# Two transformer blocks in one kernel: the residual stream of the second expert pass, the output projection and the FFN accumulated with tokens instead of features on the partitions

## The reference, cut to what matters

```python
# first block, end: PEER experts, then the final norm of the block
act = gelu(einsum("td,thkd->thk", xb, expert_down[idx]))
x = x + einsum("thk,thkd->td", gate * act, expert_up[idx])
x = rmsnorm(x, norm_final_w)
# second block
h = rmsnorm(x, attn_norm)
mq, mk, mv, rq, rk, rv, rg = split(h @ w_in)          # attention and retention
x = x + concat([moba_out, ret_out]) @ w_out
h = rmsnorm(x, ffn_norm)
u = causal_dwconv(h @ w_up, conv_w, conv_b)           # FFN, D_FF = 2816
x = x + (gelu(u) * (h @ w_gate)) @ w_down
g = sigmoid(rmsnorm(x, ple_norm) @ w_ple_gate)
x = x + (p @ w_ple) * g                               # embedding, gated
return rmsnorm(x, final_norm)
```

## Time and profile before

| | us |
|---|---|
| median of 3 runs | 1421.46 (1421.29 to 1421.8) |
| the profiled execution | 1424.04 |
| its span, first to last instruction | 1422.2 |
| TensorE busy in the span | 1352.4 |
| VectorE / ScalarE / GpSimd busy | 981.9 / 718.3 / 505.2 |
| mean granted TensorE clock | 0.985 |

### The profile page before, as it was taken

The page is one execution under the profiler, slowest core; times in us unless marked ns, Lnnn a source line. Parts: engine busy times, 40 slices in busy tenths (PEclk is TensorE's granted clock), DMA queues, the critical chain, the costliest instruction groups (busy, mean ns, idle before and its releaser), DMA issues.

```text
span 1422.2 us, 29762 instructions
## 1 busy us (share of the span) xinstructions
PE 1352.4 (95%) x11009; PEld 1325.3 (93%) x11009; DVE 981.9 (69%) x1832; ACT 718.3 (51%) x1040; POOL 505.2 (36%) x274
## 2 busy tenths in 40 slices
PE   5989999999999999999999999999999989999986
PEld 5889989999999999999999999999888879999986
DVE  6767567999898477765666666666676667666665
ACT  4842445777777743334444444444544445444443
POOL 1000000878768777777888777000000000000000
PEclk9999999999999999999999999999999998999998
DMA  6970333666566755556777677666543334445522
GB/s 247 382 307 1 119 124 145 182 178 180 171 179 180 196 158 146 126 140 189 211 206 200 199 203 211 230 231 232 186 175 119 119 118 148 179 178 182 190 104 89
DMA packets 89234, 251.00 MB, mean 176 GB/s; under 512 B 40992, under 2 KB 57504, under 8 KB 62416
## 3 DMA queue, kind: packets, MB, share of 16 engines
q1 hardware_dynamic: 47424, 229.23, 45.6%
q0 software_dynamic: 41744, 20.90, 9.7%
HBM read 232.14 MB, written 17.96 MB: 176 GB/s over the span
## 4 chain that ended last, share of the span: by engine, by line
PE 82%; DVE 7%; ACT 4%; DMA 3%; issue 3%; ACTq 0%; SPq 0%; DVEq 0%
PE ps L413 25%; PE ps L414 25%; PE ps L415 25%; DMA raw<-in_wts 3%; PE ps L825 2%; DVE wlo L409 1%; ACT whi L396 1%; DVE h L556 1%; ACT L1150 1%; PE ps L521 1%; PE ps L769 1%; PE ps L688 1%; DVE alo L577 0%; PE ps L677 0%; ACT L396 0%
## 5 line engine op out<-in xcount | busy, mean ns | idle before, releaser
L409 DVE TENSOR_TENSOR wlo<-raw,whi 128x1024 fp32r<-128x1024 f32 x412 | 502.6, 1222 | 182.5 <-ACT whi L396 156.6
L396 ACT ACTIVATE whi<-raw 128x1024 fp32r<-128x1024 f32 x412 | 435.0, 1057 | 346.0 <-PE ps L415 296.1
L413 PE MATMUL ps<-ahi,whi 128*128 128x256 f32 x2016 | 583.1, 289 | 18.7 <-DVE alo L577 9.1
L414 PE MATMUL ps<-alo,whi 128*128 128x256 f32 x2016 | 573.6, 285 | 0.0
L415 PE MATMUL ps<-ahi,wlo 128*128 128x256 f32 x2016 | 573.1, 284 | 0.0
L377 POOL DMA_INDIRECT gates_dense<-gate,spot x256 | 494.5, 1932 | 196.9 <-issue 89.7
L413 PEld LDWEIGHTS ps<-ahi,whi 128*128 128x128 f32 x2016 | 390.4, 194 | 26.6 <-issue 16.8
L414 PEld LDWEIGHTS ps<-alo,whi 128*128 128x128 f32 x2016 | 390.3, 194 | 0.3 <-issue 0.2
L415 PEld LDWEIGHTS ps<-ahi,wlo 128*128 128x128 f32 x2016 | 389.8, 193 | 0.0
L413 PE MATMUL ps<-phi,whi 128*128 128x256 f32 x1200 | 339.4, 283 | 2.0 <-DVE plo L1618 2.0
L414 PE MATMUL ps<-plo,whi 128*128 128x256 f32 x1200 | 339.1, 283 | 0.0
(11 more groups left out here) (330 smaller groups left out, 1018.0 us busy)
## 6 DMA issues: line engine op xcount, KB each, us to landing
raw<-in_wts SPq DMA_DIRECT2D x206, 1024.0 KB
gates_dense<-pf POOLq DMA_DIRECT2D x4, 4096.0 KB, 17.3
gd<-gates_dense SPq DMA_DIRECT2D x22, 256.0 KB
gd<-gates_dense SPq DMA_DIRECT2D x10, 512.0 KB
gates_dense<-gate,spot POOLq DMA_INDIRECT x256
cst<-in_c POOLq DMA_DIRECT2D x1, 1216.0 KB, 12.6
x<-in_x_t SPq DMA_DIRECT2D x1, 1024.0 KB, 4.9
kk<-in_keys POOLq DMA_DIRECT2D x1, 1024.0 KB, 5.1
```

The lines of the kernel that those rows point to most:

```text
L396: nc.scalar.activation(whi[:, j, :], raw_tile(j // 2, j % 2), ACT.Copy).then_inc(s["w_hi"], 1)
L409: nc.vector.tensor_tensor(wlo[:, j, :], raw_tile(j // 2, j % 2), whi[:, j, :].bitcast(F32), ALU.subtract).then_inc(s["w_lo"], 1)
L413: nc.tensor.matmul(out_ap, wh, xh, start=first, stop=False, skip_group_check=True)
L414: nc.tensor.matmul(out_ap, wh, xl, start=False, stop=False, skip_group_check=True)
```

## The change

What follows is what the edit does on each engine.

- The expert pass, the second output projection, FFN down, the embedding and the gate use a new `token_rows`: result 128 tokens x 512 features in a bank, stationary 128 tokens of the activation, moving 512 columns of the weight, 12 matmuls for a tile. `tokens(tb)` is the slice of token block tb. The residual in banks 4 to 7 is now token-major: bank 4 + 2 tb + half. In the gated part the embedding is made the same way, half of it ahead of the FFN (tile `W_PLE`) and half behind (tile `W_PLE2`), and so is the gate (`rows_of` instead of `columns`).
- `seed` puts the first block's x into the banks with 128-column matmuls against the identity, four for a bank instead of one of 512.
- Norms: ScalarE squares a row of tokens and sums it in the same instruction (`accum_out`), so the sums over features lie on the partitions; the inverse root is a column (`r_col`) with which the next copy or result is scaled. `turn` transposes the token-major x into PSUM (16 transposes for a norm), and `turned_act`, `turned_dve` make `ahi` and `alo` from there.
- The last tiles are walked bank by bank: the last two of the expert pass (banks 4, 6, then 5, 7) and of the output projection, the last of FFN down, the last three of the gate. x leaves a bank while the next one is still being added up.
- A 1 MB table of the two final norm weights in rows (`wrow`) is loaded by GpSimd's queue at the end of the expert pass. The output is token-major and leaves in four pieces as before.

```diff
+            def token_rows(b4, j, xh, xl, halves=range(4), first=False, last=False):
+                for b0 in halves:
+                    c = slice(b0 % 2 * 512, (b0 % 2 + 1) * 512)
+                    m = products(bank(b4 + b0, 512), xh[:, tokens(b0 // 2)], xl[:, tokens(b0 // 2)],
+                                 whi[:, j, c], wlo[:, j, c], first, last)
+                return m
+            def turn(n, src, q, tbs=range(TB)):
+                for k in (2 * q, 2 * q + 1):
+                    for tb in tbs:
+                        m = nc.tensor.transpose(bank(TURN_BANK[n][q], P, base=k % 2 * T + tb * P),
+                                                src[:, tb, k * P:(k + 1) * P], ident[:, :])
+                return m
-            with pe.Fori(0, N_EXP // 4) as i:
+            with pe.Fori(0, N_EXP // 4 - 1) as i:
                 for n in range(4):
                     pe.wait_ge(s["w_lo"], i * 4 + (W_UP + n + 1))
                     pe.wait_ge(s["p_split"], i * 4 + (n + 1))
-                    add_outer(n, phi[:, n % 2, :], plo[:, n % 2, :])
+                    token_rows(4, n, phi[:, n % 2, :], plo[:, n % 2, :]).then_inc(s["w_used"], 1)
...
+            pe.wait_ge(s["w_lo"], W_V2)
+            pe.wait_ge(s["p_split"], N_EXP)
+            for b0 in BY_HALF:
+                if b0 == 3:
+                    pe.wait_ge(s["xa"], 1)
+                    pe.wait_ge(s["xd"], 1)
+                    for q in range(2):
+                        turn(3, xt, q).then_inc(s["turned"], 1)
+                for n in range(N_EXP - 2, N_EXP):
+                    m = token_rows(4, n % 4, phi[:, n % 2, :], plo[:, n % 2, :], (b0,))
+                if b0 != 3:
+                    m.then_inc(s["x_ps"], 1)
+            m.then_inc(s["w_used"], 2)
...
+        def turned_act(act, n, q, weight):
+            act.wait_ge(s["turned"], TURNED[n] + q + 1)
+            act.wait_ge(s["w_used"], USED_BEFORE[n])
+            for k in (2 * q, 2 * q + 1):
+                m = nc.scalar.activation(ahi[:, k, :], turned_at(n, k), ACT.Copy, scale=weight(k))
+            m.then_inc(s["src_hi"], 1)
...
+            embedding(W_PLE, 0).then_inc(s["emb_ps"], 1)
+            pe.wait_ge(s["ya"], 1)
+            for q in range(2):
+                turn(5, h32_t, q, (0,))
+            embedding(W_PLE, 1).then_inc(s["w_used"], 1)
...
+            act.wait_ge(s["x_ps"], 5)
+            A(sq_t[:, 0, :], bank(4, D), ACT.Square, accum_out=ss[:, 2, 0:1]).then_inc(s["t_sq"], 1)
+            act.wait_ge(s["t_sq"], 5)
+            A(root[:, 2, 0:1], ss[:, 2, 0:1], ACT.Sqrt, scale=1.0 / D, bias=eps).then_inc(s["t_root"], 1)
...
-            for n in range(KT):
-                u = W_PLEG + n
-                pe.wait_ge(s["w_lo"], u + 1)
-                if n >= 2:
-                    pe.wait_ge(s["ple_gate"], n - 1)
-                gemm_tile(pe, u % 4, bank(n % 2, T), 6 if n == 0 else None)
-            norm_pe(pe, 6)
+            for b0 in range(4):
+                for k in range(5, KT):
+                    if b0 == 0:
+                        pe.wait_ge(s["w_lo"], W_PLEG + k + 1)
+                    m = token_rows(0, (W_PLEG + k) % 4, ahi[:, k, :], alo[:, k, :], (b0,), last=k == KT - 1)
+                m.then_inc(s["gate_ps"], 1)
```

More of the change, by code:

```diff
@@ new lines, in _ @@
+            pe.wait_ge(s["w_lo"], W_PLE2 + 1)
+            embedding(W_PLE2, 0).then_inc(s["emb_ps"], 1)
+            pe.wait_ge(s["xa"], 3)
+            pe.wait_ge(s["xd"], 3)
+            for q in range(2):
+                turn(6, xt, q).then_inc(s["turned"], 1)
+            embedding(W_PLE2, 1).then_inc(s["w_used"], 1)
+            pe.wait_ge(s["xa"], 4)
+            pe.wait_ge(s["xd"], 4)
+            for q in range(2, 4):
+                turn(6, xt, q).then_inc(s["turned"], 1)
+            for k in range(5):
+                u = W_PLEG + k
+                pe.wait_ge(s["w_lo"], u + 1)
+                if k % 2 == 0:
+                    pe.wait_ge(s["operand"], 4 * 6 + k // 2 + 1)
+                for b0 in range(4):
+                    if k == 0 and b0 == 2:
+                        pe.wait_ge(s["emb_d"], 2)
+                    if k == 0 and b0 == 3:
+                        pe.wait_ge(s["emb_a"], 2)
+                    m = token_rows(0, u % 4, ahi[:, k, :], alo[:, k, :], (b0,), first=k == 0)
+                m.then_inc(s["w_used"], 1)
@@ new lines, in _ @@
+            hi_for(W_PLEG)
+            A(warm[:, 3:4], ones[:, 0:1], ACT.Sqrt)
+            for tb in range(TB):
+                act.wait_ge((s["xa"], s["xd"])[tb], 4)
+                row_squares(3, tb, xt[:, tb, :])
+            act.wait_ge(s["t_sq"], 9)
+            A(root[:, 3, :], ss[:, 3, 0:TB], ACT.Sqrt, scale=1.0 / D, bias=eps).then_inc(s["t_root"], 1)
+            for n in range(1, KT):
+                hi_for(W_PLEG + n)
+            A(warm[:, 4:5], ones[:, 0:1], ACT.Sigmoid)
+            act.wait_ge(s["t_r"], 5)
@@ L1818, in _ @@
-            norm_dve(dve, ch, 6, 3)
+            lo_for(W_PLE2 - 1)
+            dve.wait_ge(s["x_ps"], 8)
+            x_out(2)
+            dve.wait_ge(s["w_used"], W_PLE2)
+            x_out(3)
+            lo_for(W_PLE2)
+            dve.wait_ge(s["emb_ps"], 2)
+            V.tensor_copy(emb[:, 1, :], bank(2, 512)).then_inc(s["emb_d"], 1)
+            for q in range(4):
+                turned_dve(dve, 6, q, ple_weight)
+            lo_for(W_PLEG)
+            dve.wait_ge(s["t_root"], 5)
+            V.reciprocal(r_col[:, 4, :], root[:, 3, :]).then_inc(s["t_r"], 1)
```

450 lines of the change are left out of this document (267 added, 183 removed).

## The result

The changed kernel takes 1382.86 us (median of 4 runs, 1380.92 to 1384.92) beside 1421.63 us for the kernel before (4 runs, 1421.29 to 1422.51): a ratio of 0.9727, 95% interval 0.971 to 0.9743. It is 38.8 us faster where 51.6 were forecast, and its time lies 0.9 us above the top of the range. The profiled execution took 1383.61 us around a span of 1381.8 us, 40.4 us less than the span of before.

The account below looks back on a forecast made before the run. TensorE's work plus the stretches in which it has none was taken as the bound. Savings of 26.5 + 3.9 + 7.4 + 9.6 + 4.2 = 51.6 us from 1421.46 gave 1369.9 us, range 1362 to 1382.

Parts of the forecast that it names:

- Matmuls: 168 tiles going from 24 matmuls of 256 columns to 12 of 512 save 0.159 us each, 26.5 us taken.
- After the expert pass: From the last two expert tiles through q and k, overhead falls from 10.3 to 6.4 us: 3.9 us saved.
- Ahead of the FFN: Between output projection and FFN, overhead with the new norm falls from 12.0 to 4.6 us: 7.4 us saved.
- Ahead of the gate: From last down tile through the gate, no square sum stands in the way, 1.8 us of transposes remain: 9.6 us saved.
- behind it: From the gate's end to the program's end, 9.1 us against 13.3: 4.2 us saved.
- Claimed at nothing: Seed, the split of the embedding's input and the 1 MB table were put at no cost.
- Scatters hold the weights: Rival: in the expert pass GpSimd's scatters land 10 us late, weights and TensorE 5 us late, 1375 us; chance 0.15.
- New norms are queues: Rival: at three places TensorE waits 2 us more each, half clock follows twice, 9 us lost, about 1380 us; chance 0.15.
- Columns alone count: Rival: the expert pass gains nothing from wide matmuls, 25.1 us saving is left, 1396 us; chance 0.05.
- Half clock in the pass: Rival: wide matmuls bring half clock in the expert pass, 5.1 us a tile; 1466 us if 40 tiles; chance 0.03.

Follow-up runs that it names:

- phi_on_64: The changed kernel with phi and plo laid directly behind alo, so that they start on a multiple of 64 bytes; 1378.3 us.
- halves: phi_on_64 with each matmul of 512 columns issued as two of 256 with the same stationary operand; 1396.02 us.
- ahi_32_behind: The changed kernel with ahi and alo 32 bytes behind a multiple of 64, phi and plo unchanged; 1373.7 us.
- before_ahi_32: The kernel before with ahi and alo 32 bytes behind a multiple of 128, all else as it was; 1410.24 us, ratio 0.9919.
- phi_32_behind: The changed kernel with phi and plo behind alo as in phi_on_64, but 32 bytes later; 1379.95 us.
- both_layouts: gates_later with ahi and alo 32 bytes behind a multiple of 64, which pushed phi to 64 bytes behind a multiple of 128; 1372.41 us.
- same_32: The changed kernel with whi, wlo, phi and plo all 32 bytes behind a multiple of 128, ahi and alo on one; 1373.21 us.
- gates_later: phi_on_64 with SyncE's wait for the last scatter moved behind the next two weight loads, some gates read from other experts; 1374.0 us.
- weights_32_behind: The changed kernel with whi and wlo 32 bytes behind a multiple of 128, and ahi and alo 64 behind; 1370.34 us.
- before_phi_64: The kernel before with phi and plo on a multiple of 64 bytes; 1422.43 us against 1422.57.

## Why the prediction missed, point by point

- **Matmuls, 26.5 us: this is the step that failed.** It took V's 0.2269 us for every wide matmul. The number was right for V, whose operands begin alike, and 7.6 ns short for `phi`, whose start is 96 bytes off that of the weights: 128 expert and 22 down tiles x 12 x 0.0076 = 13.7 us. That leaves 12.8 of this term's 26.5; the rest of the sum, 25.1 us, came out 0.9 us (by the medians) to 2.5 us (by the two profiled executions) better than forecast. Neither 0.1067 + 0.0135 nor 0.2133 + 0.0135 us is a constant of the form. The clue was open before the run: V was the only example, and the text said that V is short, but it did not ask in what else V differs from the pass.
- **After the expert pass, 3.9 us: right in kind, low by about 1.** The wait for `plo` came where it was forecast (2.06 us against 2.2), but the 1.6 us at half clock did not follow; overhead 4.9 us for 6.4. That was luck: in six of the nine traces with this 2.06 us wait the half clock does follow.
- **Ahead of the FFN, 7.4 us: right, low by about 1.** The FFN starts 5.5 us behind the projection's last matmul (1157.36 - 1151.86), of which 2.7 are embedding; 6.3 were forecast. The last wait was 0.71 us, not 1.7, so the walk priced the quarters too high.
- **Ahead of the gate, 9.6, and behind it, 4.2 us: right.** 13.9 us and 4.2 us of saving in the table above where 14.1 and 4.2 were forecast; TensorE has no pause over 0.5 us in that stretch, and 9.1 us follow it.
- **Claimed at nothing:** the attention lost 1.1 us to a stretch at half clock behind the 1.61 us pause. The row of before with the same pause and full clock was read as safe; it is not: in eight of the fourteen traces of this study the half clock follows this pause.
- **Scatters hold the weights:** not in the changed kernel (0.3 us), whose tiles took 2.81 us. Once they take 2.72, in phi_on_64, SyncE waits 10.2 us and TensorE 7.46; the rival had both the place and the mechanism, and its 5 us were too little in that execution. The faster tiles are not all of it: the last scatter began 4.0 us later there (877.16 us) than in the changed kernel (873.19 us), though the pass began 3.1 us earlier. Near the end a scatter and its 0.3 us fill exactly a tile: 2.51 + 0.30 in the changed kernel, 2.42 + 0.30 in phi_on_64. But not every scatter of the pass does. GpSimd in the changed kernel:

```profile
856.32 1.54 POOL L401 DMA_INDIRECT gates_dense<-gate,spot  x1 [0.30 <-issue]
...
867.57 2.51 POOL L401 DMA_INDIRECT gates_dense<-gate,spot  x1 [0.30 <-issue]
```

Of the 80 that begin behind 660 us, 24 take under 1.6 us, though VectorE does the same work beside them. The Trainium skill, "SBUF — State Buffer", section "Who interferes with whom", says that a `tensor_tensor` takes none of what descriptors need, by which the scatters would not depend on it, and also that a VectorE instruction with two inputs in SBUF contends with a GpSimd instruction that reads SBUF, by which they could. The long scatters speak for a tie to the tile, the short ones against a plain hold. What holds a scatter for the length of a tile was not tried.
- **New norms are queues:** no; the new norms cost less than walked.
- **Columns alone count:** no; halves shows that the number of matmuls is what the pass gains from. The 2.5 ns beyond its columns that the Trainium skill, "TensorE: Matmul & The Clock Gate", section "Back-to-back issue gap", gives for an isolated matmul at full clock is not what this stream pays: 120.0 - 106.7 and 226.7 - 213.3 ns are 13 ns in either form.
- **Half clock in the pass:** it came in phi_on_64, but behind a pause of 7.46 us; with the pause gone the wide stream kept 1.00.

The range was the forecast's own working plus queues and scatters; no case in it stood for "the wide form is a little slower in the pass than in V", between the forecast and columns alone, and that case was the outcome. No rival that was written down was the cause.

## What to carry to other kernels

Before a rate measured in one stage is priced into another, list everything that differs, the byte offsets of both operands included: here 32 to 96 bytes of padding decided 13 us, and a table of starts next to the table of paces showed it. When the wide form is meant to replace the narrow one, begin the stationary and the moving operand alike (the pairs here agreed modulo 512 bytes); where the narrow form with 256 columns stays, try them unlike. And after removing time from a pipelined pass, look again at the slowest side chain with a fixed end, here the scatters, which cost 0.3 us of wait in the changed kernel and took back most of the gain at once. Two executions of the same instructions reached the pass 4 us apart here, so an effect of 2 us is read from stretches of the traces, not from the times.

## What the runs showed of the hardware

- A stream of 512-column fp32r matmuls, each with its own weight load, runs at 0.2267 us when both operands begin alike (0 and 0, 32 and 32 bytes behind a multiple of 128), and at 0.2333 to 0.2343 us in the six unlike pairs of the table. The like pairs agreed modulo 512 bytes as well, so which multiple decides is open; 64 is too small. With 256 columns it is the other way: 0.1200 us with both on a boundary, 0.1167 to 0.1183 us in the unlike pairs. The Trainium skill, "SBUF — State Buffer", section "Who interferes with whom", gives TensorE two independent read ports, one for the moving operand and one for the weight load. These runs do not show how the ports work, only that the pace depends on both addresses together. Open: the narrow pass of the kernel before, with `phi` 96 bytes off `whi`, stays at 0.120 us and does not share the gain. A pair does not fix the narrow pace either: with `ahi` 32 bytes off, q and k take 0.1167 us in ahi_32_behind and 0.1178 in before_ahi_32.
- Whether the clock falls behind a pause of 1.6 to 2.1 us at full clock is not decided by its length. The 2.06 us wait for `plo` stands in nine traces: in phi_on_64, phi_32_behind, ahi_32_behind, both_layouts, same_32 and halves the half clock follows, in the changed kernel, gates_later and weights_32_behind it does not. The pause of 1.59 to 1.67 us in the attention stands in all fourteen: full clock behind it in the kernel before, before_phi_64, before_ahi_32, phi_32_behind, weights_32_behind and halves, half clock in the other eight. What decides stays open. phi_32_behind, with steps of 0.43 us where the changed kernel has 0.23:

```profile
1003.48 0.66 PE L440 MATMUL ps<-whi,phi 128*128 128x512 f32 x1 [2.06 <-DVE plo L1784]
...
1005.23 0.63 PE L441 MATMUL ps<-wlo,phi 128*128 128x512 f32 x1
1005.65 0.63 PE L442 MATMUL ps<-whi,plo 128*128 128x512 f32 x1
```

- The runs of phi_on_64 range over 6.6 us, and GpSimd's last scatter starts anywhere from 864 us (both_layouts) to 877 us (phi_on_64), so a kernel that leaves it no slack may vary more; that the one comes from the other is not shown.
